# The expert block of a hybrid decoder layer on one core: weights stationary before, tokens stationary after

## What is computed

```python
gu = xb @ w_gate_up[e] + b_gate_up[e]
gate = jnp.minimum(gu[:, 0::2], SWIGLU_LIMIT)
up = jnp.clip(gu[:, 1::2], -SWIGLU_LIMIT, SWIGLU_LIMIT)
hidden = (up + 1.0) * gate * jax.nn.sigmoid(SWIGLU_ALPHA * gate)
return hidden @ w_down[e] + b_down[e]
```

## Time and profile before

| | us |
|---|---|
| median of three runs | 2373.13 (2368.89 to 2374.94) |
| the profiled execution | 2372.35 |
| its span, first to last instruction | 2370.5 |
| TensorE busy in it | 2273.3 (96%) |
| VectorE, ScalarE, GpSimd busy | 941.1, 460.3, 225.1 |
| granted TensorE clock, mean | 0.981 |

### The profile page before, as it was taken

One profiled execution on the slowest core, in us unless ns is written; L12 is line 12 of the kernel. 1 busy time (PEld: TensorE's weight loads), 2 busy tenths in 40 slices (PEclk: granted clock), 3 DMA queues, 4 the chain that ended last, 5 costly groups with the idle time before them and its releaser, 6 DMA issues.

```text
span 2370.5 us, 43566 instructions
## 1 busy us (share of the span) xinstructions
PE 2273.3 (96%) x17841; PEld 2164.4 (91%) x17842; DVE 941.1 (40%) x2192; ACT 460.3 (19%) x848; POOL 225.1 (9%) x172
## 2 busy tenths in 40 slices
PE   6999999999969999999999999999999999999997
PEld 5878888777869999999999999999999999999997
DVE  6434434875363333233333333433333332333332
ACT  4243143664101111111111111111111111111110
POOL 1101101100000100001010001100010110001001
PEclk9999999999979999999999999999999999999998
DMA  4222222105378887788888877886888886888882
GB/s 163 98 71 72 89 89 65 62 2 186 114 234 265 270 284 237 236 272 268 288 277 288 278 239 248 274 278 220 289 271 283 271 265 216 286 290 272 287 271 36
DMA packets 250615, 504.05 MB, mean 213 GB/s; under 512 B 7994, under 2 KB 36718, under 8 KB 250238
## 3 DMA queue, kind: packets, MB, share of 16 engines
q1 hardware_dynamic: 234268, 451.96, 54.9%
q0 software_dynamic: 14912, 45.71, 9.7%
q10 hardware_dynamic: 1344, 5.01, 0.7%
HBM read 469.46 MB, written 31.10 MB: 211 GB/s over the span
## 4 chain that ended last, share of the span: by engine, by line
PE 91%; DVE 4%; issue 3%; DMA 1%; ACT 0%; POOL 0%; DVEq 0%; ACTq 0%; SPq 0%; POOLq 0%
PE bank L1053 43%; PE bank L1064 19%; PE bank L804 12%; PE bank L1041 3%; DVE hx L1413 2%; PE bank L1012 2%; PE bank L921 2%; PE bank L908 2%; PE bank L956 1%; PE bank L958 1%; PE bank L957 1%; PE bank L1004 1%; PE bank L886 1%; PE bank L812 1%; PE bank L898 0%
## 5 line engine op out<-in xcount | busy, mean ns | idle before, releaser
L1053 PE MATMUL bank<-hx,ring 128*128 128x140 f32 (+1 forms) x8192 | 1037.6, 288 | 26.2 <-issue 16.7
L1053 PEld LDWEIGHTS bank<-hx,ring 128*128 128x128 f32 x8192 | 1021.4, 197 | 33.2 <-issue 32.2
L1064 PE MATMUL bank<-hx,ring 128*128 128x140 f32 (+1 forms) x4096 | 514.7, 287 | 0.0
L1064 PEld LDWEIGHTS bank<-hx,ring 128*128 128x128 f32 x4096 | 507.0, 190 | 0.0
L760 ACT ACTIVATE hx<-hx 128x168 f32<-128x168 f32 x256 | 87.9, 343 | 1447.0 <-DVE hx L1484 1447.0
L1484 DVE TENSOR_SCALAR hx<-bank,hx 128x168 f32<-128x168 f32 x256 | 100.4, 392 | 639.4 <-PE bank L1053 638.9
L1509 DVE TENSOR_SCALAR hx<-bank,hx 128x168 f32<-128x168 f32 x256 | 100.5, 392 | 353.8 <-PE bank L1064 353.8
L573 POOL DMA_INDIRECT out_x<-mix,hx x66 | 99.8, 1513 | 825.4 <-ACT mix L753 780.9
L552 POOL DMA_INDIRECT mix<-xn_scratch,hx x66 | 64.7, 981 | 718.8 <-DVE hx L1408 708.7
L804 PE MATMUL bank<-hx_r,mix_r 128*128 128x512 f32 x480 | 116.1, 401 | 7.9 <-DVE hx_r L1147 7.9
L804 PEld LDWEIGHTS bank<-hx_r,mix_r 128*128 128x128 f32 x480 | 92.1, 193 | 28.4 <-issue 9.2
(11 more groups left out here) (202 smaller groups left out, 1697.8 us busy)
## 6 DMA issues: line engine op xcount, KB each, us to landing
ring<-in_w_gate_up SPq DMA_DIRECT2D x128, 2048.0 KB, 10.8
ring<-in_w_down SPq DMA_DIRECT2D x64, 2048.0 KB, 8.8
mix<-in_w_in SPq DMA_DIRECT2D x14, 1024.0 KB, 5.0
work<-in_w_in SPq DMA_DIRECT2D x14, 1024.0 KB, 5.0
ring<-in_x SPq DMA_DIRECT2D x8, 512.0 KB, 8.2
hx<-in_w_out SPq DMA_DIRECT2D x1, 4096.0 KB, 14.1
work<-in_x ACTq DMA_DIRECT2D x8, 512.0 KB, 4.8
out_x<-work SPq DMA_DIRECT2D x8, 512.0 KB, 4.4
```

The lines of the kernel that those rows point to most:

```text
L1053: mm = e.matmul(bank[f % 2][:, part * CAP:part * CAP + w], gu_ring[:, k, f * 256 + part:(f + 1) * 256:2], xT[:, k, 0:w], start=k == 0, sto ...
L1064: return e.matmul(bank[2 + j % 2][:, 0:w], dn_ring[:, k, j * P:(j + 1) * P], hid[:, k, 0:w], start=k == 0, stop=k == KD - 1)
```

## The change

The block is turned round: **tokens are stationary and weights stream**. The tokens' transpose (128x128 per slice of the model width) is the stationary operand, and a 512-column piece of a weight row block is the moving one, accumulated in four banks for gate/up and two for down. Results have the token on the partition. What goes with it:

- Gate/up is taken in eight chunks of 128 weight rows (1 MB, `raw_slot`), down in four chunks of 256 rows; six raw slots for twelve chunks. Each gate/up chunk and down chunks 2 and 3 are split by ScalarE into an upper fp32r half (`upper`) and by VectorE into the remainder (`lower`), 128x2048 elements each, ten pairs for a block; then three fp32r matmuls stand for one fp32 matmul. Down chunks 0 and 1 (`RAW_D = 2`) are used in plain fp32.
- A raw slot is loaded again when `lower` has read its chunk and, where TensorE reads it raw, when those matmuls are done (`load_next`).
- Up to 128 tokens a block has no more than that. With 129 to 160 tokens, the up to 32 further tokens are handled in plain fp32 in four column groups of the array: four matmuls of a 128x32 stationary with 512 different weight columns each (gate/up) or 256 (down), each writing its own 32 partitions of one bank. A block holds 160 tokens, not 168, so the expert with 165 gets a second block: 33 blocks.
- Biases are added by a bf16 matmul with a selector of the expert's row (three bf16 parts). The ffn norm's gain is applied before the rows are stored, on VectorE; the router's tokens are copied by ScalarE.
- The activation now runs after the last gate/up chunk, bank by bank: sigmoid (ScalarE), clip of up, product, product with clipped gate (VectorE); the hidden rows are then turned back by TensorE (ten 128x128 transposes), copied or split, and are the stationary operand of down. The output needs no transpose.

Cut to its core (the functions replaced are those printed above):

```diff
-CAP = 168
-HC = CAP // 2
+OV = 32
+GR = P // OV
+CAP = P + OV
...
-WIDTHS = (140, CAP)
+RAW_D = 2
+NSP = KD + 4 - RAW_D
+HS = 5
+RS = 6
+NC_E = KD + 4
...
+        raw_slot = [region(ring, 2048 * (c % RS), 2048) for c in range(NC_E)]
+        low_slot = [region(deep_r, 2048 * i, 2048) for i in range(4)] + [region(ring_r, 12288, 2048)]
+        up_slot = [region(hx_r, 2048 * i, 2048) for i in range(4)] + [region(ring_r, 14336, 2048)]
...
+            def load_next(n, c, x_e):
+                before_it = c + RS if c < RS else c - RS
+                past = 1 if c < RS else 0
+                if before_it < KD:
+                    e.wait_ge(c_lo, n * NSP + (before_it + 1 - past * NSP))
+                    e.sem_inc(sp_go, 1)
+                elif before_it >= KD + RAW_D:
+                    e.wait_ge(c_lo, n * NSP + (before_it - RAW_D + 1 - past * NSP))
+                    e.sem_inc(sp_go, 1)
+                e.wait_ge(c_raw, n * NC_E + (before_it + 1 - past * NC_E))
+                load_chunk(c, x_e)
...
+            def upper(n, c):
+                chunk = c if c < KD else c + RAW_D
+                e.wait_ge(c_in[chunk], n * 16 + 16)
+                e.wait_ge(c_use, n * NSP + (c + NSP - HS + 1))
+                e.activation(up_slot[c % HS], raw_slot[chunk], ACT.Copy).then_inc(c_hi, 1)
...
+            def block_act(n):
+                upper(n, 0)
+                upper(n, 1)
+                tokens_up(n)
+                upper(n, 2)
+                weigh_rows(n)
+                for c in range(3, KD + 2):
+                    upper(n, c)
+                sigmoids(n, 0)
+                sigmoids(n, 1)
+                hidden_up(n, 0)
+                sigmoids(n, 2)
+                hidden_up(n, 1)
+                sigmoids(n, 3)
+                hidden_up(n, 2)
+                sigmoids(n, 4)
+                hidden_up(n, 3)
+                hidden_up(n, 4)
+                for c in range(KD + 2, NSP):
+                    upper(n, c)
...
+            def gate_up(n, k, over):
+                hi, lo = up_slot[k % HS], low_slot[k % HS]
+                terms = ((xT_hi[:, k], hi), (xT_lo[:, k], hi), (xT_hi[:, k], lo))
+                last = k == KD - 1
+                def main(b, t):
+                    return e.matmul(bank[b][:, :], terms[t][0], terms[t][1][:, b * CH:(b + 1) * CH], start=False,
+                                    stop=last and t == 2, skip_group_check=True)
+                def ride():
+                    for j in range(GR):
+                        mo = e.matmul(bank[4][quarter_rows(j), :], xo[:, k % 2, OV * (k // 2):OV * (k // 2 + 1)],
+                                      raw_slot[k][:, j * CH:(j + 1) * CH], start=False, stop=last, skip_group_check=True)
+                    mo.then_inc(c_raw, 1)
+                e.wait_ge(c_hi, n * NSP + (k + 1))
+                if last:
+                    if over:
+                        ride()
+                    e.wait_ge(c_lo, n * NSP + (k + 1))
+                    for b in range(4):
+                        for t in range(3):
+                            mm = main(b, t)
+                        mm.then_inc(m_gu, 1)
+                else:
+                    for t in range(3):
+                        if t == 2:
+                            e.wait_ge(c_lo, n * NSP + (k + 1))
+                        for b in range(4):
+                            mm = main(b, t)
+                    mm.then_inc(c_use, 1)
+                    if over:
+                        ride()
...
+            def down_terms(d, c):
+                k, s = 2 * d + c, slice(c * D, (c + 1) * D)
+                if d < RAW_D:
+                    return ((hT_raw[:, k], raw_slot[KD + d][:, s]),)
+                i, k = (KD + d - RAW_D) % HS, k - 2 * RAW_D
+                hi, lo = up_slot[i][:, s], low_slot[i][:, s]
+                return ((hT_hi[:, k], hi), (hT_lo[:, k], hi), (hT_hi[:, k], lo))
...
+            def down_over(n, d):
+                if d >= RAW_D:
+                    e.wait_ge(c_in[KD + d], n * 16 + 16)
+                for c in range(2):
+                    for j in range(GR):
+                        mm = e.matmul(bank[7][quarter_rows(j), 2 * P:4 * P], ho[:, c, OV * d:OV * (d + 1)],
+                                      raw_slot[KD + d][:, c * D + j * 2 * P:c * D + (j + 1) * 2 * P],
+                                      start=False, stop=d == 3 and c == 1, skip_group_check=True)
+                mm.then_inc(c_raw, 1)
+            def block_matmuls(n, over):
+                e.wait_ge(s_sel, n + 1)
+                e.wait_ge(x_hi_ok, n * 5 + 5)
+                e.wait_ge(x_lo_ok, n * 4 + 4)
+                gate_up_bias(over)
+                for k in range(KD):
+                    gate_up(n, k, over)
+                    if k == 5:
+                        e.wait_ge(l_hot, n + 2)
+                        e.wait_ge(l_ok, n + 1)
+                        e.wait_ge(m_y, n * 3 + 3)
+                        token_list()
+                e.wait_ge(l_ok, n + 2)
+                down_bias(over)
+                turn_hidden(n, 0)
+                turn_hidden(n, 1)
+                down_main(n, 0, over)
+                turn_hidden(n, 2)
+                turn_hidden(n, 3)
+                turn_hidden(n, 4)
+                down_main(n, 1, over)
+                if over:
+                    e.wait_ge(h_hi, n * 5 + 5)
+                    down_over(n, 0)
+                    down_over(n, 1)
+                e.wait_ge(g_in, n * 32 + 64)
+                turn_tokens(n)
+                for d in range(2, 4):
+                    if over:
+                        down_over(n, d)
+                    down_main(n, d, over)
...
+            def lower(n, c):
+                e.wait_ge(c_hi, n * NSP + (c + 1))
+                chunk = c if c < KD else c + RAW_D
+                e.tensor_tensor(low_slot[c % HS], raw_slot[chunk], up_slot[c % HS].bitcast(F32), ALU.subtract).then_inc(c_lo, 1)
...
+            def hidden(n, b):
+                e.wait_ge(m_su, n * 5 + (b + 6))
+                if b in (2, 3):
+                    e.wait_ge(m_ht, n * 5 + (b - 1))
+                dst = hid_o if b == 4 else hid[:, b % 2]
+                e.scalar_tensor_tensor(dst, bank[b][:, 0:CH:2], GLIM, su[:, b % 2], ALU.min, ALU.mult).then_inc(m_hid, 1)
+            def hidden_low(n, b):
+                e.wait_ge(h_hi, n * 5 + (b + 1))
+                m = 2 * (b - RAW_D)
+                e.tensor_tensor(hT_lo[:, m:m + 2], bank[b][:, 0:2 * P].rearrange("p (c t) -> p c t", c=2),
+                                hT_hi[:, m:m + 2].bitcast(F32), ALU.subtract).then_inc(h_lo, 1)
+            def block_dve(n):
+                lower(n, 0)
+                lower(n, 1)
+                tokens_low(n)
+                lower(n, 2)
+                lower(n, 3)
+                e.wait_ge(l_sum, n + 1)
+                after = e.value_load(it_i[0:1, 0, bass.ds(n + 1, 1)], min_val=0, max_val=NE)
+                list_hot(n + 1, after)
+                lower(n, 4)
+                lower(n, 5)
+                lower(n, 6)
+                e.wait_ge(l_ok, n + 1)
+                e.wait_ge(m_y, n * 3 + 3)
+                e.wait_ge(sc_done, n * 32 + 48)
+                e.tensor_copy(idx_sc, idx)
+                e.tensor_copy(w_sc, wsel).then_inc(l_keep, 1)
+                e.wait_ge(l_keep, n + 1)
+                e.wait_ge(l_sum, n + 2)
+                list_out(n + 1)
+                for c in range(7, KD + 2):
+                    lower(n, c)
+                up_part(n, 0)
+                up_sig(n, 0)
+                for b in range(5):
+                    if b < 4:
+                        up_part(n, b + 1)
+                    hidden(n, b)
+                    if b < 4:
+                        up_sig(n, b + 1)
+                    if b > RAW_D:
+                        hidden_low(n, b - 1)
+                for c in range(KD + 2, NSP):
+                    lower(n, c)
+                e.wait_ge(s_dn, n + 1)
+                expert_sel(after)
```

516 lines of the change are left out of this document (262 added, 254 removed).

## The result

The changed kernel takes 2583.12 us (median of 4 runs, 2581.78 to 2586.99), the kernel before 2372.2 us beside it: ratio 1.0892, 95% interval 1.0874 to 1.0911. The forecast was 2620 us in 2480 to 2800, slower by 10%. The profiled execution has a span of 2581.4 us; its terms can be laid beside the sum 2617.

The account below looks back on a forecast made before the run. The prediction took TensorE's stream, 91% of the chain and mostly plain fp32 expert matmuls, as the bound. Start 686, blocks 1880, jump 37 and end 14 gave a 2617 us span, forecast 2620 us, 10% slower, range 2480 to 2800.

Parts of the forecast that it names:

- Holes: TensorE idle around the activation and down in each block: 9.1 us narrow, 7.4 us wide.
- TensorE's work: Matmuls and transposes of a block: 38.6 us narrow, 51.8 wide; by work alone the change gains 134 us.
- The second pair: TensorE idle after the first transposes, while ScalarE and VectorE prepare the next hidden rows: 2.0 us a block.
- The first hole: TensorE idle after gate/up and bias, with lower halves standing before the activation: 3.9 us narrow, 2.4 wide.
- Clock: TensorE's clock falls at the first hidden pair in every block, at the second in most: 3.0 us a block.
- The loop's jump: TensorE stands 2.2 us for issue behind some 14 of 18 wide blocks; with two further cases, 37 us.
- Changes around the router: Element-wise work moves between engines with several us of slack per token tile: costs 0.
- The block table's part: Before the first block, 9.8 us of VectorE table work, then 4.6 and 1.9, put the first loop matmul at 686.
- Column groups that do not overlap: Rival: the four groups overlap only in twos, 2805 us, or not at all, near 3180; chance 0.12.
- The clock low through the down half: Rival: half clock from gate/up to down's split half costs 7 instead of 3 us a block: 2750 us; chance 0.10.
- Shorter holes: Rival: late lower halves do not delay the first pair and the clock holds: 2420 us; chance 0.15 for 2390 to 2520.
- faster: the work is what counts: Rival: matmul work covers the activation, holes near 0 at full clock: 2250 us, faster below 3.7 us lost a block; chance 0.06.

Follow-up runs that it names:

- e_woven: e_order with the splits of down's two split chunks, and one weight-chunk split by the token halves, moved to where ScalarE and VectorE wait: 2303.8 us.
- e_order: The changed kernel with only the hidden phase reordered on TensorE, ScalarE and VectorE, the first down chunk running after bank 0's turn: 2490.1 us.
- e_nogroups: The changed kernel with every block on the narrow path, leaving out an expert's tokens past 128: 2392.3 us, single time.
- e_late: The changed kernel with the splits of down's two split chunks moved behind the activation on ScalarE and VectorE: 2436.0 us.
- e_fill: The changed kernel with 36 unused matmuls a block added in TensorE's holes, nothing else changed: 2525.4 us.
- e_same: The changed kernel with all four matmuls of a set sent to one column group instead of four: 3065.9 us, single time.
- e_both: The changed kernel with both the edits of e_order and those of e_late: 2421.3 us.

## Why the prediction was right, and where it was not

The direction, the size and most terms held; the span is 36 us under the sum (2581.4 against 2617). One block, predicted and measured, in us. Holes are idle time of TensorE; lost clock is half of the time for which it is busy at half clock; work is a block of e_woven less its idle time:

| | work | holes | lost clock | block |
|---|---|---|---|---|
| narrow, predicted | 38.6 | 9.1 | 3.0 | 50.7 |
| narrow, measured | 39.3 | 8.5 | 2.7 | 50.5 |
| wide, predicted | 51.8 | 7.4 | 3.0 | 62.2 |
| wide, measured | 53.7 | 5.7 | 2.7 | 62.0 |

So the block times are nearly exact in part by luck: too little work and too much waiting cancel, by about 2 us in a wide block. By the steps:

**TensorE's work**: right in its prices, a little short in the sum. The set of four at 1.00 us was the value taken. The 38.6 us of a narrow block are 39.3: TensorE is busy for 38.4 to 39.1 of 40 us in the windows of e_woven, and a block takes 40.5 with about 1.2 idle. bf16 matmuls of 512 columns, taken at the fp32r price, are 0.88 / 4 = 0.22. Too small was the wide block's surplus of 13.2: 14.5 between the blocks of e_woven. The missing part fits the change of shape: from the first gate/up matmul to the token list, six chunks take 16.53 us in a narrow block of e_woven and 23.68 in a wide one, (23.68 - 16.53) / 6 = 1.19 us a set, 0.19 beyond its own 1.00.

**Holes**: 9.1 and 7.4 us predicted. Measured as idle time, without the length of the matmul ahead of each hole: 4.85 + 1.54 + 1.54 + 0.56 = 8.5 in a narrow block, 2.03 + 1.54 + 1.54 + 0.56 = 5.7 in a wide one. The second pair (2.0 predicted, 1.54), bank 3 (2.0, 1.54) and the groups' rows (1.0, 0.56) came for the reasons given; e_order removed them and left the smaller ones named there. By the prediction's own sign, 4 to 7 us idle between the last gate/up and the first plain down matmul, narrow blocks are right with 6.4 and wide ones just outside with 3.6. The first hole had the right place, the late splits ahead of the activation, but "waiting about 0.7 for the upper half of a chunk whose slot came free late" is an upper half that waits for a landing: the transfer, 10.68 us long in the block shown, begins at 1823.78, when VectorE has just freed its slot. The 2.4 of the wide block (2.0 measured) I read as what is left when the groups hide some of the hole. They do hide 3 us, as e_nogroups shows, but what made the hole was a queue order that could be undone, as e_late showed. The start of the narrow block's hole, 24.5 us, was slightly off: the prediction's own terms give 18.1 + 5.5 + 0.5 = 24.1, and 24.2 is measured.

**Clock**: 3.0 us a block taken. Every block is at 0.50 for some time, in most of them in one stretch of 6.8 us that spans the first turns, the second hole and most of the first down chunk. TensorE is busy for 5.3 us of it in a wide block and 5.5 in a narrow one, so 2.7 us are lost; 2.6 came back in e_fill's wide blocks.

**The loop's jump, 37 us: the step that failed.** I carried the 2.20 us of issue behind a wide block over at "that rate", 14 of 18. In the kernel after there is none: behind every block the next bias matmul starts 0.23 us after the last down matmul did. I had a row for the size and none for the condition. The profile's pages point at one, in the queue that carries instructions (packets, MB, share), the first row of the kernel before, the second of the kernel after:
```profile
q8 instruction: 76, 1.25, 0.2%
q8 instruction: 40, 0.66, 0.1%
```
In the kernel before, 36 of them fall between 745 and 2250 us: they run while it is in a wide block or just behind one, and there are none over long runs of narrow blocks (750 to 890, 1200 to 1360 us). Each of the four stands behind a wide block has such a transfer 1.6 to 1.7 us ahead of it (945.3 us ahead of the stand at 947.03); the end of the fifth wide block, near 1008 us, has none ahead of it since 949.9, and no stand. In the kernel after that queue has none from 745 us to the last block, though it changes between its two paths too. TensorE leaves some 860 records of matmuls and weight loads in a block of the kernel before on either path, 353 and 628 in the kernel after. That the stand was TensorE waiting for instructions that have to be loaded again, and that the shorter program does without, fits all this; no run tried it, so the cause stays open.

**Changes around the router, 0: also wrong.** "Several us of slack per token tile" was true of each engine's busy time and not of the queue: the bias split on ScalarE sat between two steps that TensorE waits for. The first block started at 694.3 instead of 686. The block table's part (9.8 + 4.6 + 1.9) was no worse than that: with the bias moved the start is 685.2.

**The end**: the last block starts at 2517.9; with a narrow block's 50.5 it leaves 13 us to 2581.4, against 14 in the sum. Together, 8 us more at the start, 6 less in the blocks, 37 less at the jump and 1 less at the end are the 36 us.

**The rivals.** Column groups that do not overlap: e_same shows what they would have cost, 3066 us against the 3180 worked out. The clock low through the down half did not come: the last three of the first chunk's eight matmuls start 0.43 us apart again where the first five had 0.85, and the second chunk is at 3.44. The Trainium skill (TensorE: Matmul & The Clock Gate, HAM oscillation) tells of bursts that each start cold; the trace agrees for the first chunk behind the holes, 5.46 us for 3.44, and e_fill shows that matmuls of no use are a way to hold the clock. "Shorter holes" and "faster: the work is what counts" were forecasts of a kernel one or a few edits away. The kernel that the first describes, without the first hole and with the clock mostly held, is e_late with 2436 us for the 2420 given; that e_both has 2421 is chance, since it has other holes. The second put the turning point at 3.7 us of holes and lost clock a block and its time at 2250; e_woven is left with 1 to 2 us in narrow blocks (40 us less the 38.4 to 39.1 busy) and takes 2304, under the kernel before as the rival had it, though 54 us above its number. The floor of 39.5 us by transfers for a narrow block was worked out too and is nearly reached: 40.5 at a DMA share of 0.82 to 0.93.

So where did the expected gain of 134 us of TensorE work go? About 45 us of it were never there (0.7 us of work more in a narrow block and 1.9 in a wide one). The rest went into 6 to 8.5 us of idle time a block and into a clock that fell behind it, and nearly all of both came from the order in which three engines take their queues: 1.2 to 1.3 us of holes and no lost clock are left in e_woven. With the same instructions, woven, the change gains 3%.

## What to carry to other kernels

When a tensor stage is shortened by moving its post-processing behind it, write down each helper engine's queue in the order it executes and ask of every long item ahead of the critical one when its result is needed; here two splits ahead of the activation, not needed yet, cost 147 us. Put such items where the engine waits for TensorE anyway, rather than at either end. Price a TensorE hole of about 2 us or more at its own length plus what the half clock behind it took here (1.4 to 5 us; behind those of up to 1.2 us in e_woven it took nothing), and when a price is carried over from a trace, name the condition under which it occurred there.

## What was not expected of the hardware

- A stand of 1.96 us behind dense fp32r matmuls was followed by 10.2 us at 0.50 of the clock (604.6 to 614.8), one of 2.07 us in the expert block by 6.8 (1437.4 to 1444.2). What came behind them differed too: transposes and the router's narrow matmuls ahead of the dense ones in the first case, two transposes, another hole and down's matmuls in the second. How long the clock stays low is not read off the hole's length alone.
- In e_late every block has the same three holes (1.54, 1.54 and 0.56 us), and the clock fell in 14 of the 33 blocks. The same order of work can come out either way.
- fp32 matmuls of 512 columns in four different column groups, 1.00 us a set, against 3.55 in one group: 3.55 times. The Trainium skill (TensorE: Matmul & The Clock Gate, Measured speedup vs the span model) has 2.38 for three tiles, and the estimate of 1.1 us from it was too high. To each set comes about 0.2 us in the full-width matmuls behind it.
- A transfer of 1 MB, 5.4 us from issue to landing in the median, took 9.7 to 11.9 for chunk 11 in narrow blocks of the changed kernel and 4.5 to 5.1 in wide ones. In the narrow block shown the four down chunks are issued at 2.2, 5.7, 10.4 and 12.6 us from its first bias matmul and are in flight together; in the wide one shown, at 13.4, 17.3, 21.3 and 25.2, each has landed before the next but one is issued. That the crowding is the cause was not tried.
